# Fewer joined orders between ACT, DVE and TensorE, pool products on high and low halves, and half a weight chunk between the variance's sums, in a two-block kernel (a three-branch block, then an S5 and a gated-linear-attention layer)

## The reference, cut to what matters

```
# block 1
h = rmsnorm(x, norm_g);  a_u, a_v, a_z, b_p, b_z, c_h, c_b, c_c, c_z, gates = split(h @ w_in)
ya = spatial_gating(gelu(a_u), gelu(a_v), ...) * silu(a_z)
d  = window_mean(b_p, (2, 4, 8, 16)) - b_p                       # four groups of 256 columns
yb = (einsum('bsgc,gcd->bsgd', d, pool_w) + pool_b) * pool_scale * silu(b_z)
yc = c_b * conv3(c_c * c_h) * silu(c_z)
x  = rmsnorm(x + (sigmoid(g0)*(ya@w_a) + sigmoid(g1)*(yb@w_b) + sigmoid(g2)*(yc@w_c)) @ w_out, final_g)
# block 2, layer 0
a_in, a_z, b_val, b_gate, b_z = split(rms_norm(x) @ ev_w_in)
ya = gelu(s5_layer(a_in)); ya = ya * sigmoid(ya @ w_glu + b_glu) * silu(a_z)
c  = depthwise_conv31(b_val * sigmoid(b_gate))                   # causal
yb = (silu(layer_norm(c)) @ w_pw + b_pw) * silu(b_z)
x  = x + rms_norm(concat(ya, yb) @ ev_w_out)
# block 2, layer 1: gated linear attention with 4 heads, then x = x + rms_norm(...)
```

## Time and profile before

| | before |
|---|---|
| median of 3 runs (lowest to highest) | 1674.43 us (1673.84 to 1678.49) |
| profiled execution, time and span | 1676.68 us, 1674.7 us |
| TensorE busy | 1635.3 us, 98% of the span |
| VectorE (DVE), ScalarE (ACT), GpSimd (POOL) busy | 972.2, 672.4, 203.3 us |
| mean granted clock of TensorE | 0.995 |
| moved by DMA | 207.32 MB, mean 124 GB/s |

### The profile page before, as it was taken

The page is one execution under the profiler, slowest core; times in us unless marked ns, Lnnn a source line. Parts: engine busy times, 40 slices in busy tenths (PEclk is TensorE's granted clock), DMA queues, the critical chain, the costliest instruction groups (busy, mean ns, idle before and its releaser), DMA issues.

```text
span 1674.7 us, 19670 instructions
## 1 busy us (share of the span) xinstructions
PE 1635.3 (98%) x7688; PEld 1356.0 (81%) x7688; DVE 972.2 (58%) x1350; ACT 672.4 (40%) x943; POOL 203.3 (12%) x234
## 2 busy tenths in 40 slices
PE   6999999999999999998999999999999999999998
PEld 5888898878888888887898888877887878878886
DVE  4267164544235423456899999874474636465457
ACT  5333233233221223334454544566255435353253
POOL 3990000000000000003122220212000000000000
PEclk9999999999999999999999999999999999999999
DMA  8463533243333333234888895679322222222311
GB/s 253 124 188 113 136 104 126 76 151 88 103 99 96 96 98 99 91 101 144 244 164 205 190 191 171 146 176 232 115 63 89 78 86 89 64 82 69 99 52 63
DMA packets 151438, 207.32 MB, mean 124 GB/s; under 512 B 52043, under 2 KB 75067, under 8 KB 150331
## 3 DMA queue, kind: packets, MB, share of 16 engines
q1 hardware_dynamic: 132123, 174.15, 34.0%
q0 software_dynamic: 17568, 29.89, 10.8%
q10 hardware_dynamic: 1664, 2.13, 0.4%
HBM read 191.46 MB, written 14.68 MB: 123 GB/s over the span
## 4 chain that ended last, share of the span: by engine, by line
PE 92%; DVE 3%; ACT 2%; DMA 2%; issue 1%; SPq 0%; ACTq 0%; DVEq 0%
PE PS L2341 80%; PE PS L2319 3%; PE PS L2633 2%; PE PS L2583 1%; PE PS L2499 1%; PE PS L2450 1%; PE PS L2466 1%; DMA T<-d_tm 1%; DMA WL<-in_conv_w_pw_dram 1%; PE PS L2599 0%; PE PS L2623 0%; PE PS L2437 0%; ACT WH L945 0%; PE PS L2573 0%; PE PS L2704 0%
## 5 line engine op out<-in xcount | busy, mean ns | idle before, releaser
L2341 PE MATMUL PS<-HH,WH 128*128 128x512 f32 x1216 | 475.3, 391 | 5.8 <-DVE HL L1497 3.0
L2341 PE MATMUL PS<-HL,WH 128*128 128x512 f32 x1216 | 473.8, 390 | 0.0
L2341 PE MATMUL PS<-HH,WL 128*128 128x512 f32 x1216 | 473.7, 390 | 0.0
L945 ACT ACTIVATE WH<-WR 128x1024 fp32r<-128x1024 f32 x200 | 211.5, 1061 | 625.2 <-PE PS L2341 590.7
L1473 DVE TENSOR_TENSOR WL<-WR,WH 128x1024 fp32r<-128x1024 f32 x144 | 185.2, 1296 | 413.1 <-ACT WH L945 412.8
L2341 PEld LDWEIGHTS PS<-HH,WH 128*128 128x128 f32 x1216 | 228.7, 188 | 55.6 <-issue 5.9
L2341 PEld LDWEIGHTS PS<-HH,WL 128*128 128x128 f32 x1216 | 228.7, 188 | 47.6
L2341 PEld LDWEIGHTS PS<-HL,WH 128*128 128x128 f32 x1216 | 228.7, 188 | 47.3 <-issue 0.2
L1880 DVE SCALAR_TENSOR_TENSOR TMP<-CP,PRM,TMP 128x512 f32<-128x512 f32 x232 | 155.2, 742 | 0.0
L2341 PE MATMUL PS<-WH,HH 128*128 128x512 f32 x352 | 139.6, 396 | 4.9 <-DVE WL L1473 4.0
L2341 PE MATMUL PS<-WL,HH 128*128 128x512 f32 x352 | 138.3, 393 | 0.0
(11 more groups left out here) (388 smaller groups left out, 2092.5 us busy)
## 6 DMA issues: line engine op xcount, KB each, us to landing
WR<-in_w_in_dram SPq DMA_DIRECT2D x96, 512.0 KB, 3.7
WR<-in_od_w_in_dram SPq DMA_DIRECT2D x32, 512.0 KB, 3.9
WR<-in_ev_w_in_dram SPq DMA_DIRECT2D x24, 512.0 KB, 5.0
WL<-in_ev_w_in_dram POOLq DMA_DIRECT2D x24, 512.0 KB, 7.8
WR<-in_ev_w_in_dram SPq DMA_DIRECT2D x32, 256.0 KB, 3.4
WR<-in_ev_w_out_dram SPq DMA_DIRECT2D x16, 512.0 KB, 4.2
WR<-in_od_w_in_dram SPq DMA_DIRECT2D x32, 256.0 KB, 3.4
WR<-in_od_w_out_dram SPq DMA_DIRECT2D x16, 512.0 KB, 3.8
```

Of the source, the lines that this page charges most:

```text
L945: act.activation(WH[:, n % RING, :, :], WR[:, n % RING, :, :], ACT.Copy).then_inc(w_hi, 1)
L2341: mm = pe.matmul(out_banks[m], st, mv, start=(kt == 0 and i == 0), stop=(kt == 2 * per - 1 and i == 2))
```

## The change

It has these parts:

- **Pool.** ACT rounds `pool_w` into `PWH` and DVE writes `PWL` over the raw copy; `U` (the pool's input) gets halves in `YH`, `YL`. TensorE makes three fp32r products for each one. The conversions are placed between g1's weight chunks. The reload of `X` moves on SP's queue behind section c_h and the pool.
- **Splits of four, parted.** On ACT, at a_u.1, g0.0 and g0.1, three chunks are copied ahead of the evacuation and one behind it; on DVE the layer norm's steps stand between pairs of chunks. SP loads b_p.0 ahead of the stores of `d_wt`.
- **u_t.** DVE normalises tile 2 behind the last tile's addition, and `turned("u_t.0")` (the four `HL`) comes ahead of the split of b_vg.0's second chunk. `free_bank` waits for a single low half.
- **Tables.** The second halves of `VT` and `T6` are loaded in two pieces each, the second with semaphores of its own, awaited at pair 24.
- **Moments.** The first half of ev_a.1's third chunk goes between the second and third sum of squares.
- **pw.** ACT converts pw's chunks one group of `z_silu` earlier; SP loads pw.1 ahead of `X1`.
- **Tail.** The last output tile is scaled and stored in two halves.

```diff
+        PWH = put("PWH", "R3", [4, 2, 256], F32R, skip=8192)
+        PWL = put("PWL", "R6", [4, 2, 256], F32R)
@@ SP
+            unit("b_p.0", w_in, W_IN["b_p"])
             sp.wait_ge(banks_act, act_after("w_t.1"))
...
-            section("b_p", w_in, W_IN["b_p"])
+            unit("b_p.1", w_in, W_IN["b_p"] + NC)
...
-            sp.wait_ge(d_ready, 4)
+            section("c_h", w_in, W_IN["c_h"])
+            sp.wait_ge(side_done, side_after("pool.1"))
             sp.wait_ge(s5_out, 16 * S5_OUT)
             sp.dma_start(X[:, :, :], x_d).then_inc(x_again, 16)
-            section("c_h", w_in, W_IN["c_h"])
-            sp.wait_ge(side_done, side_after("pool.1"))
...
-            vt_in_half(1)
-            t6_in_half(1)
+            tables_in(0, 8, vt_in, t6_in)
+            tables_in(8, 8, vt_rest, t6_rest)
...
             unit("pw.0", a["conv_w_pw_2"][0], 0)
+            unit("pw.1", a["conv_w_pw_2"][0], NC)
             sp.wait_ge(side_done, side_after("moments"))
             sp.dma_start(X1[:, :, :], tokens(d_x1)).then_inc(x1_in, 16)
...
-            unit("pw.1", a["conv_w_pw_2"][0], NC)
@@ ACT
-            split()
+            split(3)
             evac("a_u.1", [U[:, 4 + m, :] for m in range(4)], ACT.Gelu_apprx_tanh)
+            split(1)
...
-            split()
+            split(3)
             act.wait_ge(v_done, 4)
             evac("g0.0", [G[:, m, :] for m in range(4)], ACT.Sigmoid)
             wts_out(1)
-            split()
+            split(1)
+            split(3)
             evac("g0.1", [G[:, 4 + m, :] for m in range(4)], ACT.Sigmoid)
+            split(1)
...
             evac("b_z.0", [CH[:, m, PPAD:] for m in range(4)], ACT.Silu)
-            split()
+            split(1)
+            act.wait_ge(pw_in, 16)
+            act.wait_ge(s5_out, 16 * S5_OUT)
+            for i in range(2):
+                act.activation(PWH[:, 2 * i:2 * i + 2, :, :].rearrange("p g k n -> p (g k n)"),
+                               PW[:, 2 * i:2 * i + 2, :, :].rearrange("p g k n -> p (g k n)"), ACT.Copy).then_inc(pw_hi, 1)
+            act.wait_ge(weights_used, used_after("w_a.1"))
+            y_halves(d_ready, lambda kt: kt // 2 + 1, lambda kt: U[:, kt, :], range(4))
+            split(1)
+            y_halves(d_ready, lambda kt: kt // 2 + 1, lambda kt: U[:, kt, :], range(4, 8))
+            split(2)
             evac("b_z.1", [CH[:, 4 + m, PPAD:] for m in range(4)], ACT.Silu)
...
             act.activation(BNA[:, 3, 0:1], EPS[:, 0:1], ACT.Silu)
+            split(1)
...
             evac("ev_a.1", [YO[:, m, NC:D] for m in range(4)], ACT.Copy)
-            split()
+            split(3)
@@ DVE (its pool conversions, two subtractions and eight YL, stand between g1's chunks as ACT's do)
                 if t == 2:
                     scaled(1, 7, std2, XN1, xn1)
                     split(1)
+                if t == 3:
                     scaled(2, 7, std2, XN1, xn1)
             scaled(TT - 1, 7, std2, XN1, xn1)
+            turned("u_t.0", 0, "norm_pre0", 2)
             split(1)
-            turned("u_t.0", 0, "norm_pre0", 2)
@@ TensorE
-                a, d = JOBS[i - 2][3:5]
-                if (a, d) == (4, 0):
+                a, d, lo = JOBS[i - 2][3:]
+                if lo:
+                    pe.wait_ge(h_lo, lo[1] - 3 + m)
+                elif (a, d) == (4, 0):
...
-                    pe.wait_ge(d_ready, g + 1)
+                    pe.wait_ge(y_lo, 8 + 2 * g + 2)
                     for k in range(2):
-                        mm = pe.matmul(bank(f"pool.{i}", m), PW[:, g, k, (kt % 2) * P:(kt % 2 + 1) * P], U[:, 2 * g + k, :],
-                                       start=(k == 0), stop=(k == 1))
+                        for j, (wi, ai) in enumerate(halves):
+                            mm = pe.matmul(bank(f"pool.{i}", m), (PWH, PWL)[wi][:, g, k, (kt % 2) * P:(kt % 2 + 1) * P],
+                                           Y(2 * g + k)[ai], start=(k == 0 and j == 0), stop=(k == 1 and j == 2))
...
+                    if pr == 24:
+                        pe.wait_ge(vt_rest, 16)
+                        pe.wait_ge(t6_rest, 16)
...
             for k in range(KT // 2):
+                if k == 2:
+                    ev_a(1, (2,), (0,))
                 pe.wait_ge(summed_up, 2 + k)
                 mm = pe.matmul(bank("moments", 1), ONES[:, :], SQ[:, 2 * k, :], start=(k == 0), stop=(k == KT // 2 - 1))
             mm.then_inc(side_done, 1)
-            ev_a(1, (2, 3))
+            ev_a(1, (2,), (1,))
+            ev_a(1, (3,))
```

More of the change, by code:

```diff
@@ L412, in three_branch_s5_gla_kernel @@
         cpads = sem("cpads")
-        x1_done, xn1, sq1, std1, sq2, std2 = (sem(n) for n in (
-            "x1_done", "xn1", "sq1", "std1", "sq2", "std2"))
+        x1_done, xn1, std1, std2 = (sem(n) for n in (
+            "x1_done", "xn1", "std1", "std2"))
         states, conv_done = sem("states"), sem("conv_done")
@@ L1099, in _ @@
             evac("b_z.0", [CH[:, m, PPAD:] for m in range(4)], ACT.Silu)
-            split()
+            split(1)
[9 more added lines that the diff above has]
+            split(2)
             evac("b_z.1", [CH[:, 4 + m, PPAD:] for m in range(4)], ACT.Silu)
-            act.wait_ge(weights_used, used_after("w_a.1"))
             y_halves(yb_ready, lambda kt: kt + 1, lambda kt: CH[:, kt, PPAD:], range(8))
@@ L1660, in _ @@
             split()
-            split()
+            split(1)
+            for i in range(2):
+                dve.wait_ge(pw_hi, i + 1)
+                w, hi = PW[:, 2 * i:2 * i + 2, :, :], PWH[:, 2 * i:2 * i + 2, :, :]
+                dve.tensor_tensor(PWL[:, 2 * i:2 * i + 2, :, :].rearrange("p g k n -> p (g k n)"),
+                                  w.rearrange("p g k n -> p (g k n)"), hi.rearrange("p g k n -> p (g k n)").bitcast(F32),
+                                  ALU.subtract).then_inc(pw_lo, 1)
+            y_low(1, lambda kt: U[:, kt, :], range(4))
+            split(1)
+            y_low(1, lambda kt: U[:, kt, :], range(4, 8))
+            split(2)
             for i in range(2):
@@ L2251, in last_norm @@
                 dve.wait_ge(yg_done, 2 * t + 2)
-                dve.scalar_tensor_tensor(YO2[:, t, :], YG2[:, t, :], STAT[:, 3, t:t + 1], X1[:, t, :], ALU.mult, ALU.add).then_inc(fin, 1)
+                for cols in ([slice(0, D)] if t < TT - 1 else [slice(0, NC), slice(NC, D)]):
+                    dve.scalar_tensor_tensor(YO2[:, t, cols], YG2[:, t, cols], STAT[:, 3, t:t + 1], X1[:, t, cols],
+                                             ALU.mult, ALU.add).then_inc(fin, 1)
             for t in range(TT):
@@ L2328, in unit @@
                     low_ready(n0 + q)
-                    for kk in range(2):
+                    for kk in kks:
                         kt = 2 * q + kk
@@ L2470, in _ @@
             section("c_h", H, ready(h_lo, 0))
-            section("w_b", Y, ready(y_lo, 1))
+            section("w_b", Y, ready(y_lo, 2))
             section("c_c", H, ready(h_lo, 0))
@@ L2475, in _ @@
             section("c_z", H, ready(h_lo, 0))
-            section("w_c", Y, ready(y_lo, 2))
+            section("w_c", Y, ready(y_lo, 3))
             section("w_out", H, ready(h_lo, 1), rows=True, by_tile=True)
@@ L2522, in _, with ev_a @@
                                   for m in range(4)])
-            section("glu", Y, ready(y_lo, 3))
-            def ev_a(u, chunks):
+            section("glu", Y, ready(y_lo, 4))
+            def ev_a(u, chunks, kks=(0, 1)):
                 unit(chunks_before(f"ev_a.{u}"), [bank(f"ev_a.{u}", m) for m in range(4)], H,
                      ready(h_lo, 3) if u == 0 else (lambda kt: None), True, tile, chunks=chunks,
-                     bank_ready=lambda m: free_bank(f"ev_a.{u}", m))
+                     bank_ready=lambda m: free_bank(f"ev_a.{u}", m), kks=kks)
             ev_a(0, (0, 1, 2, 3))
@@ L2540, in _ @@
             mm.then_inc(side_done, 1)
-            ev_a(1, (2, 3))
-            section("pw", Y, ready(y_lo, 4))
+            ev_a(1, (2,), (1,))
+            ev_a(1, (3,))
+            section("pw", Y, ready(y_lo, 5))
             section("ev_b", H, ready(h_lo, 4), rows=True, by_tile=True, units=(0,))
```

34 lines of the change are left out of this document (23 added, 11 removed).

## The result

After: 1660.34 us (median of 4 runs, 1659.53 to 1662.08); before: 1674.99 us (4 runs). The ratio is 0.991, with a 95% interval of 0.9893 to 0.9928: 14.7 us, 0.9%, faster. A later series gave 1659.51 us for the changed kernel (5 runs, against 1675.99; 0.9901, 0.9886 to 0.9916). The forecast was 1658.0, with a range of 1654.5 to 1664.0.

The account below looks back on a forecast made before the run. TensorE, busy 98% of the span, was taken as the bound. Terms summed to 17.5 us: 1659.2 from the profiled 1676.7, 1656.9 from the median; 1658.0 was taken, range 1654.5 to 1664.

Parts of the forecast that it names:

- u_t's addition: Before u_t: the last w_out tile's addition no longer waits for XN of tile 2, so everything up to tile 3's transposes is 0.5 earlier.
- Pool products: At the pool: 48 fp32r products and g1's first take 11.13 us instead of 13.96, operands ready in time; gain 2.8.
- The fourth weight copy: At g0.0 and a_u.1: the copy of 1.06 us no longer precedes the evacuation; gains 1.06 and 0.9, together 2.0.
- one more change from fp32 to fp32r, 0.4 by the gap 374.20 to 374.83, less 0.227: At moments: the cost set against hiding the 0.9 wait on SQ with half a chunk of ev_a.1; gain 0.4.
- u_t, order and waits by banks: At u_t: earlier addition, HL ahead of the split and waits for single HLs start b_vg.0 near 772.27; gain 2.7.
- no wait on HL comes at the fifth column block: In b_vg.0: HL 4 was forecast at 781.7, needed at 783.2; a new wait there would have shown the forecast wrong.
- I take the full clock: 3.5 x 0.49 = 1.7 us more: Behind u_t: with idle stretches of at most about 1.15 us the clock does not fall to 0.51; bounds 0 and 1.7.
- DVE is late next: At s5_y.1's tables: DVE's convolution taps run until 1038.9 before YL can begin, so the gain ends at 2.5.
- DVE then waits for TensorE again ... so the delay dies there: After u_t: X additions and HL 4 to 7 end 0.3 later, but DVE's later waiting for TensorE absorbs that delay.
- pw's weights: At pw.1: copying chunks one group earlier lands the first by 1157.3, wanted at 1159.8; wait and slow clock vanish, gain 5.0.
- Rival 1: At pw.1: the first chunk's load, sharing DMA engines, is still late; 2 to 5 us come back, 1660 to 1663; chance 0.15.
- 10 for all: At pw: an accumulating load took 10.0 us beside X1's 2 MB load, and that length was used for every such load.

Follow-up runs that it names:

- a_in first: The changed kernel with a_in.0's four weight loads issued ahead of WT's two 2 MB loads instead of behind them: 1659.54 us, ratio 0.9904 to before.

## Why the prediction was right, and where it was off

Between marks on TensorE's timeline (each stage ends at the first product of the next name), the gain in us: my terms, the two first profiles, and the second profile of before against the mean of the changed kernel's three (the sums are of unrounded values):

| stage | my terms | first profiles | second of before |
|---|---|---|---|
| start to CRAW | 0 | -2.1 | (chance) |
| CRAW to u_t (pool 2.8, copies 2.0, u_t's addition 0.5) | 5.3 | 5.4 | 5.4 |
| u_t to b_vg.0 | 2.2 | 2.1 | 2.1 |
| b_vg.0 to a_in (clock) | 1.7 | 0.6 | 0.9 |
| a_in to s5_y | 0 | -0.2 | -0.2 |
| s5_y to moments (tables) | 2.5 | 2.5 | 0.8 |
| moments to pw | 0.4 | 1.2 | 1.2 |
| pw to ev_b | 5.0 | 4.4 | 2.7 |
| ev_b to the end (tail) | 0.4 | 0.5 | 0.5 |
| sum | 17.5 | 14.4 | 13.2 |

- **Pool products**: 2.8 forecast, 2.75 read at the place in the changed kernel, 2.7 for the part alone, 2.8 at the place and 2.4 at the end when it is undone. Nothing precedes them; no wait on YL or PWL.
- **The fourth weight copy**: the wait on U (0.9) went and G's fell by 1.1, as forecast. Undone, the copies give back 2.1, 2.0 by my terms.
- **Moments**: 0.4 forecast, 1.2 measured. The step "one more change from fp32 to fp32r, 0.4 by the gap 374.20 to 374.83, less 0.227" was wrong. The gap is no price: the last fp32 record of the pool starts only 0.03 ahead of 374.20 (first line below, in before), and the 32 records at their pace of 0.427 with one fp32r product of 0.227 would take 13.89 us, where 13.96 were measured. The change costs less than 0.1. The stall on SQ cost 1.0, since TensorE's products start 1.45 apart across it and 0.43 elsewhere, and smaller pauses before it make up the rest.

```profile
374.17 0.59 PE L2466 MATMUL PS<-U,PW 128*128 128x512 f32 x1
374.20 0.80 PE L2341 MATMUL PS<-HH,WH 128*128 128x512 f32 x1
374.83 0.39 PE L2341 MATMUL PS<-HL,WH 128*128 128x512 f32 x1
```

- **u_t, order and waits by banks**: 2.7 forecast, 2.6 measured (0.6 and 2.0). The longest stall is 0.99, on the last tile's addition, where I had about 1.15; the one on HL is 0.89, and no wait on HL comes at the fifth column block.
- **The clock behind u_t**: the step "I take the full clock: 3.5 x 0.49 = 1.7 us more" and the 1.7 within pw's 5.0 took one execution's falls for the price of the waits. Over the profiles, the waits of 2.0 to 5.1 us at HL, T and pw's WL were followed by a fall in 9 of 13 cases (HL 3 of 5, T 3 of 4, WL 3 of 4). The waits do open the door to it, but the price is a mean: before's runs have a mean clock of 0.995, the changed kernel's 0.998, which over 1660 us is 4 to 5 us. My terms held 1.7 for u_t, 1.7 for pw and, unseen, about 1.6 of the tables' 2.5 (DVE's idle time is 2.45 with the fall and 0.76 without it), 5.0 in all. The sum of them was near right, and the first profile of before, with all three falls, happened to stand near its mean. That is luck: from the second profile, with one fall, the same reading would have held 1.7.
- **Tables**: the bound named ("DVE is late next") is what the runs show, and 2.5 is the idle time in that profile; from one execution to the next it is 0.8 to 3.5, and the gain between s5_y and moments follows it (2.5 and 0.8 for the two profiles of before).
- **The step that failed** is "DVE then waits for TensorE again ... so the delay dies there". For DVE it holds. But from u_t to a_in I followed DVE alone, and not the loads: a TensorE that comes 5.5 us earlier to b_vg.0 and 6.9 to a_in meets a chunk which SP issued only 0.9 us earlier behind 4 MB of WT. It costs up to 2.0 us, 0.7 on average. That term was missing, and it is gone with a_in first.
- **pw's weights**: 5.0 forecast, 4.4 between the two first profiles, 2.7 from the second of before, which had no fall there. For pw.1's first chunk the step held, with some 2 us of slack where I had 2.5. Rival 1 was right by its mechanism and wrong by its chunk: X1's load, moved behind pw.1's on SP, now starts within 0.3 us of the accumulating load of pw.0's fourth chunk, which then takes 13 us instead of "10 for all". I had listed that chunk's copy and not its load. Price: up to 0.7 of wait, where the rival had 2 to 5.
- **From the sum to the median**: I took the 2.3 us between the profiled execution and the median of three runs partly for something that leaves with the waits. Later series of before gave 1675.8, 1676.3, 1677.6 and 1676.0: the median of three lay low by chance. Their middle, about 1676.3, less 17.5, plus 0.7 for the wait in a_in, would have been 1659.5; measured were 1659.8.

The falls that come and go with the same waits fit a statement of the Trainium skill that I had not drawn on: "TensorE: Matmul & The Clock Gate", Part 1, says that the monitor which sets the clock runs on its own time and does not start anew with a kernel, so that the slow stretch at the start differs from run to run. The start agrees (transposes of 5.09 to 6.62 us); for the falls in mid-kernel no run here shows the monitor itself.

The rule that I had weighed, in the Trainium skill's "DMA: Bandwidth & Descriptors" on issuing engines, that the DMAs of all issuers interleave on the same 16 engines, is borne out at the chunk where I did not apply it: POOL's load of 512 KB for pw.0's fourth chunk landed in 12.8 to 13.5 us with SP's X1 issued 0.2 us ahead, and in 6.2 with X1 issued 18 us ahead. (WT and a_in's chunk, 13.2 us and 3.5 us, are both SP's and say nothing on it.) The same page's advice to batch to 1 MiB, which spoke against the two pieces of the tables, decided nothing: undoing the split cost 3.4 us at its place.

## What to carry to other kernels

When an edit moves the bounding engine forward, go down its list to the next transfers and ask for each when its issue moves, not only when its consumer does; what was hidden by 1 us behind a big load comes out. Do not price a fall of the clock from one profile: look at the mean granted clock of all runs, and take a part's gain at its place, in a stretch between two marks. And if two parts of work end a stall in turn (a load, then DVE's taps, then ACT), the idle time of the second is the gain of the first, in each execution anew.
